# Reordering the mixer of the second block, with GpSimd multiplying its own convolution taps

## The reference

```python
h = rms_norm(x, mix_norm[l]);  u = h @ w_in[l]          # 1024 -> 2304
u_conv, u_pool = u[..., :512], u[..., 512:768]
q, k, v = jnp.split(u[..., 768:], 3, axis=-1)           # 512 each
a, gate = split(u_conv);  z = a * sigmoid(gate)          # 256 channels
z = depthwise_conv(z, w_dw, width=31) + b_dw
y_conv = silu(layer_norm(z, ln_g, ln_b))
y_pool = multiscale_pool(u_pool, pool_w[l], pool_scale[l])   # a 256x256 matrix and a 64x64 one per group
q = rms_norm(q per head of 64); k = rms_norm(k per head of 64)
p = softmax(q k^T - slope * dist)                        # 4 heads x 2 maps of 256 x 256
o = (p[:, 0] - lam * p[:, 1]) @ v
y = concat([y_conv, y_pool, rms_norm(o) * (1 - lambda_init)]) @ w_out[l]
x = x + y
```

## Time and profile before

| | |
|---|---|
| median of 3 runs | 2148.89 us (2148.51 to 2149.14) |
| the profiled execution, its own time | 2149.96 us |
| its span, first to last instruction | 2148.1 us |
| TensorE busy | 98% of the span, mean granted clock 0.992 |
| VectorE, ScalarE, GpSimd busy | 58%, 51%, 5% |
| first `mixer2` stage in the profile | 1349.8 to 1463.9 us |
| second `mixer2` stage | 1838.0 to 1952.2 us |

### The profile page before, as it was taken

One profiled execution on the slowest core, in us unless ns is written; L12 is line 12 of the kernel. 1 busy time (PEld: TensorE's weight loads), 2 busy tenths in 40 slices (PEclk: granted clock), 3 DMA queues, 4 the chain that ended last, 5 costly groups with the idle time before them and its releaser, 6 DMA issues.

```text
span 2148.1 us, 24565 instructions
## 1 busy us (share of the span) xinstructions
PE 2097.4 (98%) x9840; PEld 1730.9 (81%) x9840; DVE 1253.8 (58%) x1609; ACT 1091.8 (51%) x1554; POOL 112.6 (5%) x128
## 2 busy tenths in 40 slices
PE   7999999999999999999999999979999999979998
PEld 6888788888888887888888888868888888868886
DVE  5555666555655556665556555676555555675554
ACT  5444564544554455554446444675444444665443
POOL 1000100000000000000000000140000000140000
PEclk9999999999999999999999999989999999989999
DMA  6554635555555554455556555525554655515553
GB/s 230 194 185 162 207 125 200 177 187 185 187 191 177 194 168 147 157 181 187 186 190 224 188 193 185 171 69 175 187 190 163 224 182 185 181 65 174 179 184 120
DMA packets 104545, 379.04 MB, mean 176 GB/s; under 512 B 11745, under 2 KB 11905, under 8 KB 104176
## 3 DMA queue, kind: packets, MB, share of 16 engines
q1 hardware_dynamic: 101808, 368.23, 51.6%
q0 software_dynamic: 2080, 8.21, 1.1%
q10 hardware_dynamic: 544, 1.05, 0.2%
HBM read 374.82 MB, written 2.62 MB: 176 GB/s over the span
## 4 chain that ended last, share of the span: by engine, by line
PE 86%; issue 9%; DVE 3%; ACT 2%; DMA 0%; POOL 0%; DVEq 0%; POOLq 0%; ACTq 0%
PE pb L333 26%; PE pb L335 26%; PE pb L334 25%; DVE scr L1297 2%; PE pb L389 2%; PE pb L352 1%; PE pb L375 1%; PE pb L427 1%; PE pb L373 1%; PE pb L374 1%; DVE wlo L1287 1%; ACT scr L1142 1%; PE pb L526 0%; ACT whi L866 0%; PE pb L500 0%
## 5 line engine op out<-in xcount | busy, mean ns | idle before, releaser
L1287 DVE TENSOR_TENSOR wlo<-raw,whi 128x1024 fp32r<-128x1024 f32 (+1 forms) x704 | 839.4, 1219 | 316.3 <-ACT whi L866 312.3
L866 ACT ACTIVATE whi<-raw 128x1024 fp32r<-128x1024 f32 (+1 forms) x704 | 716.3, 1050 | 212.3 <-PE pb L335 202.9
L333 PE MATMUL pb<-whi,XTh 128*128 128x512 f32 (+2 forms) x1904 | 751.3, 395 | 4.4 <-DVE wlo L1287 4.4
L335 PE MATMUL pb<-whi,XTl 128*128 128x512 f32 (+2 forms) x1904 | 737.6, 387 | 0.0
L334 PE MATMUL pb<-wlo,XTh 128*128 128x512 f32 (+2 forms) x1904 | 736.6, 387 | 0.0
L333 PEld LDWEIGHTS pb<-whi,XTh 128*128 128x128 f32 x1904 | 359.5, 189 | 79.6 <-DVE wlo L1287 5.9
L335 PEld LDWEIGHTS pb<-whi,XTl 128*128 128x128 f32 x1904 | 359.0, 189 | 74.3
L334 PEld LDWEIGHTS pb<-wlo,XTh 128*128 128x128 f32 x1904 | 359.7, 189 | 68.2
L333 PE MATMUL pb<-whi,HTh 128*128 128x512 f32 x816 | 321.5, 394 | 8.5 <-DVE HTl L1297 8.5
L335 PE MATMUL pb<-whi,HTl 128*128 128x512 f32 x816 | 319.2, 391 | 0.0
L334 PE MATMUL pb<-wlo,HTh 128*128 128x512 f32 x816 | 319.0, 391 | 0.0
(11 more groups left out here) (209 smaller groups left out, 1117.7 us busy)
## 6 DMA issues: line engine op xcount, KB each, us to landing
raw<-in_W SPq DMA_DIRECT2D x696, 512.0 KB, 4.2
raw<-in_W SPq DMA_DIRECT2D x8, 264.0 KB, 2.7
scratch<-scr POOLq DMA_DIRECT2D x1, 1536.0 KB, 6.4
scr<-in_bc POOLq DMA_DIRECT2D x2, 640.0 KB, 5.4
X<-in_x ACTq DMA_DIRECT2D x2, 512.0 KB, 9.1
scr<-scratch POOLq DMA_DIRECT2D x1, 1024.0 KB, 7.0
scr<-in_slope POOLq DMA_DIRECT2D x1, 1024.0 KB, 9.3
scr<-in_Pg POOLq DMA_DIRECT2D x1, 1024.0 KB, 12.5
```

Of the source, the lines that this page charges most:

```text
L333: pe.matmul(o, ah, bh, start=begin and i == 0, stop=False)
L335: ins = pe.matmul(o, al, bh, start=False, stop=end and done)
L866: return act.activation(o, i, ACT.Copy, scale=scale)
L1287: dve.tensor_tensor(wlo[u % W_SLOTS][:, 0:c], raw[u % RAW_SLOTS][:, 0:c], whi[u % W_SLOTS][:, 0:c].bitcast(F32), ALU.subtract).then_inc(*u ...
```

## The change

The groups of units are now conv, q, k, pool, v, the side batches stand elsewhere, and w_out's rows are taken in the order pool, conv, attention. The taps run from k = 6 to k = 18: VectorE two or three at each step, ScalarE three at each of the steps 6 to 10 (taps 0 to 14). Taps 15 to 30 of half 1 are multiplied and added by GpSimd alone. The root of q stands on GpSimd's queue between tap 5 and tap 6, that of k between tap 14 and tap 15. The normalisation of the convolution moves from ScalarE to VectorE (`bn_stats`, `bn_aggr`, and one instruction for subtract and multiply). The core of the diff:

```diff
-OUT2 = [2, 3, 4, 5, 6, 7, 0, 1]
+OUT2 = [2, 3, 0, 1, 4, 5, 6, 7]
+ACT_TAPS = [0, 3, 6, 9, 12, 15, 15, 15, 15, 15, 15, 15, 15, 31]
+DVE_TAPS = [0, 3, 6, 8, 11, 13, 16, 18, 21, 23, 25, 27, 29, 31]
+POOL_TAPS = range(15, 31)
+POOL_AT = (6, 15)
...
 # tensor, side(k)
+                    if k == 6:
+                        turn_pair(z, ("z", i, 1), "z", 4, ("zp", i))
+                    if k == 11:
+                        turn_head(q2, "q", 0, 5)
+                        turn_head(q2, "q", 1, 6)
                     if k == 15:
+                        turn_head(k2, "k", 0, 7)
+                        turn_head(k2, "k", 1, 4)
+                        pooled(0, 5)
+                        logits(0, 0, (6, 2))
+                        logits(0, 2, (3, 7))
+                        pooled(2, 4)
+                    if k == 16:
+                        pool_groups(4)
+                        logits(1, 0, (5, 6))
                     if k == 17:
+                        turn_pair(y[:, :, 256:512], ("pool_y", i), "pool", 7, ("pool_l", i, 1))
+                        logits(1, 2, (4, 3))
                     if k == 18:
+                        turn_maps(0, 0, 5)
+                        turn_maps(0, 2, 6)
                     if k == 19:
+                        values(0, 7)
                         turn_conv(4)
                     if k == 20:
+                        turn_maps(1, 0, 5)
+                        turn_maps(1, 2, 6)
+                        turn_pair(z, ("zn", i, 1), "zn", 4, ("conv_a", i, "yc", 1))
+                        values(1, 5)
+                    if k == 21:
+                        turn_y(0, 6)
                     if k == 22:
+                        turn_y(1, 7)
+                groups = [("z", 512, 2, 4), ("qn", 512, 2, 4), ("kn", 512, 2, 4), ("up", 256, 4, 2), ("v", 512, 2, 4)]
...
 # scalar, after step(u0 + k)
+                    if 6 <= k <= 18:
+                        tap_run(ACT_TAPS[k - 6], ACT_TAPS[k - 5])
+                    if k == 7:
+                        squares(7, 2, "q_sq2")
+                    if k == 11:
+                        turned("q", qT2, gq, 0, 5)
+                        turned("q", qT2, gq, 1, 6)
+                        squares(11, 0, "k_sq2")
+                    if k == 15:
+                        turned("k", kT2, gk, 0, 7)
+                        turned("k", kT2, gk, 1, 4)
+                        pooled(0, 5)
+                        pooled(2, 4)
                         exps(0, (0, 4, 1, 5))
...
 # vector, after step(u0 + k)
+                    if 6 <= k <= 18:
+                        tap_run(DVE_TAPS[k - 6], DVE_TAPS[k - 5])
+                    if k == 8:
+                        head_mean("q")
+                    if k == 10:
+                        head_out("q", q2, 2)
+                    if k == 12:
+                        head_mean("k")
+                    if k == 14:
+                        head_out("k", k2, 0)
+                    if k == 15:
+                        maps(0, 0, (6, 2))
+                        maps(0, 2, (3, 7))
                         maps_max(0)
+                    if k == 16:
+                        maps(1, 0, (5, 6))
+                    if k == 17:
+                        # HTl of the pool's chunks
+                        maps(1, 2, (4, 3))
                         maps_max(1)
                         maps_weights(0)
                         difference(0, 0)
                         difference(0, 2)
+                    if k == 18:
                         maps_weights(1)
                         difference(1, 0)
                         difference(1, 2)
...
 # gpsimd
+                    if j in POOL_TAPS:
+                        w.wait_ge(*at("zp", i))
+                        done = one("tap_m", i, j)
+                        pool.tensor_scalar(taps[:, j % 4, :], zp[:, 1, j:j + S], cw[:, 31 + j:32 + j], None,
+                                           ALU.mult).then_inc(*done)
+                    else:
+                        w.wait_ge(*at("tap_a", i, j))
...
-                for name in ("q", "k"):
+                at_ = 1
+                for name, to in zip(("q", "k"), POOL_AT):
+                    add_taps(i, at_, to)
+                    at_ = to
                     root(col(i, "v_" + name, 16), col(i, "r_" + name, 16), 16, (name + "2_v", i, "v"), name + "2_r", i)
-                add_taps(i, 1, 25)
+                add_taps(i, at_, 31)
+                root(col(i, "v_conv", 2), col(i, "r_conv", 2), 2, ("conv_v", i, "v"), "conv_r", i)
```

More of the change, by code:

```diff
@@ L123 @@
     tensor_reduce = tensor_tensor_reduce = tensor_tensor_scan = reciprocal = memset = dma_start = op
-    wait_ge = then_inc = op
+    bn_stats = bn_aggr = wait_ge = then_inc = op
 class Once:
@@ L820, in side @@
-                    if k == 22:
[L821 to L830, removed]
+                        turn_maps(1, 0, 5)
@@ new lines, in side @@
+                        turn_maps(1, 2, 6)
[3 more added lines that the diff above has]
+                        turn_y(0, 6)
+                    if k == 22:
+                        turn_y(1, 7)
+                groups = [("z", 512, 2, 4), ("qn", 512, 2, 4), ("kn", 512, 2, 4), ("up", 256, 4, 2), ("v", 512, 2, 4)]
+                k = 0
+                for number, (emptied, ncols, per, count) in enumerate(groups):
+                    b0 = 2 * (number % 2)
+                    for j in range(count):
+                        side(k)
+                        unit(u0 + k, [(t, b0 + t, 0, ncols) for t in range(2)], XTh, XTl,
+                             [(per * j + c, c * ncols) for c in range(per)], x_ready(n), j == 0, j == count - 1)
+                        k += 1
@@ L1170, in mixer2 @@
                     if k == 3:
[L1171 to L1178, removed]
                         w.wait_ge(*at("r", n))
                         for t in range(2):
-                            w.wait_ge(*ended(u0 + 11, t))
+                            w.wait_ge(*ended(u0 + 3, t))
@@ L1193, in mixer2 @@
+                    if k == 13:
+                        for t in range(2):
+                            w.wait_ge(*ended(u0 + 13, t))
+                            scaled(up2[:, t, :], pb[2 + t][:, 0:256], n, t).then_inc(*up("up", i, t))
+                    if k == 15:
[3 more added lines that the diff above has]
+                        pooled(2, 4)
                         exps(0, (0, 4, 1, 5))
-                        tap_run(3, 5)
+                    if k == 16:
+                        w.wait_ge(*at("pool_p", i, "y"))
+                        copy(y[:, :, 256:512], pb[4][:, :].rearrange("p (t n) -> p t n", t=2)).then_inc(
+                            *up("pool_y", i))
@@ L1207, in mixer2 @@
-                    if k == 17:
-                        turned_maps(0, 0, 7)
-                        tap_run(15, 17)
+                    if k == 17:
+                        w.wait_ge(*at("pair", i, "pool"))
+                        for c in range(2):
+                            copy(HTh[:, 2 + c, :], pb[7][:, c * S:(c + 1) * S], (gp0, gp1)[c]).then_inc(
+                                *up("pool_h", i, c))
+                        exps(1, (0, 4))
                         for t in range(2):
@@ L1220, in mixer2 @@
[L1220 to L1235, removed]
-                    if k == 19:
[L1237 to L1240, removed]
-                                           accum_out=mu[:, t:t + 1]).then_inc(*up("conv_a", i, "mu", t))
@@ L1773, in mixer2 @@
+                    if k == 17:
+                        w.wait_ge(*at("pool_h", i, 1))
+                        for c in range(2):
+                            axpy(HTl[:, 2 + c, :], pb[7][:, c * S:(c + 1) * S], (gp0, gp1)[c],
+                                 HTh[:, 2 + c, :].bitcast(F32), ALU.mult, ALU.subtract).then_inc(*up("pool_l", i, c))
+                        maps(1, 2, (4, 3))
                         maps_max(1)
-                        tap_run(7, 11)
-                    if k == 16:
@@ L2084, in layout @@
         conv, pool, q, k, v = np.split(a["w_in_2"][i], [512, 768, 1280, 1792], axis=1)
+        group(conv, 2)
         group(q, 2)
         group(k, 2)
-        group(conv, 2)
+        group(pool, 4)
         group(v, 2)
-        group(pool, 4)
         group(a["w_out_2"][i].reshape(KD, P, D)[OUT2].reshape(D, D), 1)
```

167 lines of the change are left out of this document (49 added, 118 removed).

## The result

The changed kernel takes 2161.88 us in the median of four executions (2160.11 to 2164.4) against 2148.74 us for the kernel before: a ratio of 1.0062, 95% interval 1.0044 to 1.0079. It is slower by 13 us, 0.6%. The prediction was 2157.5 us, range 2141 to 2166. The profiled execution took 2161.95 us, its span 2160.1 us: 12.0 longer than the span before.

What follows compares the result with a forecast made beforehand. TensorE bounds the kernel. Per stage, stalls 23.0, half clock 3.1 and bare work 92.3 give 118.4 us against 114.1, +8.6 for two: 2157.5 us from 2148.9, range 2141 to 2166.

Steps and rivals of the forecast that it cites:

- The wait at q: New TensorE stall of 8.8 us before the q transposes at side(11), ended by VectorE's head_out of q.
- the ring: Tap slots: ScalarE's tap 10 needs tap 6's slot, which GpSimd frees only behind q's root; ScalarE stands from 27.4 until 33.2.
- rival 1: Tap slots do not hold q back: stall of 2.6 us at side(11), 2141.7 us in all, faster; chance 0.19.
- The chain of k: TensorE stalls 4.8 us before unit 14, because the v group reuses the banks of k.
- Side(18): TensorE waits for VectorE's map differences: stall of 4.2 us, and 1.0 more for pair (0, 2).
- zn and unit 20: Stage's late part: 2.4 us of stall until zn is ready, then 0.8 after silu, copy and low part.
- The half clock: TensorE work at about half clock after the stalls at q (1.7 us) and unit 14 (1.4): 3.1 a stage.
- Bare work: TensorE's own work in a stage, without stalls and half clock: 92.3 us.
- GpSimd's multiplications: 16 taps at 0.87 us each, 1.74 with the add, hidden before turn_conv with 3.9 us to spare.
- Rival 3: GpSimd becomes the bound: at 1.6 us a multiplication turn_conv waits, 5 us more a stage, 2168 us; chance 0.09.
- rival 4: VectorE's taps wait for whole GpSimd instructions: 1.33 us a tap, 2.8 more a stage, 2163 us; chance 0.06.
- Rival 2: Clock holds at unit 14 and VectorE is 2 us earlier at side(18): 2150 us, within 0.2%; chance 0.17.

Runs made afterwards that it cites:

- Experiment 1: Changed kernel with only the root of q moved on GpSimd's queue, from behind tap 5 to behind tap 9: 2154.41 us, ratio 1.0021.
- experiment 8: Changed kernel with root of q behind tap 9, separate banks for pool and v, and VectorE's head_mean and head_out before each step's taps: 2142.02 us, 0.9966.
- experiment 4: Changed kernel with VectorE's weights and map differences of row half 0 put at the start of step 17, before the taps: 2165.45 us, 1.0072.
- experiments 9 and 10: 9, on top of experiment 8: VectorE's taps and ScalarE's splits earlier, 2145.92 us; 10, on top of 9: seven GpSimd multiplications back on ScalarE, 2144.46 us.
- experiment 2: Changed kernel with idle TensorE products, 34 before the q transposes and 18 before unit 14: 2156.8 us, ratio 1.003.
- experiment 5: Changed kernel with ScalarE multiplying all taps of half 1 again and GpSimd only adding: 2162.16 us, ratio 1.0058.
- Experiment 6: Kernel before, in its own order, with GpSimd multiplying taps 15 to 30 itself: 2167.44 us, ratio 1.0078.

## Why the prediction was right, and what it mis-sized

- **The wait at q: right, the ring's share of it too large.** 8.8 us predicted, 8.63 measured in both stages; restart 40.1 us after the stage's start predicted, 40.1 measured (1390.46 by a start of 1350.35). Experiment 1 shows that the ring makes 4.1 of it, and rival 1 (the ring doesn't hold q back) is out. Even so, rival 1's stall of 2.6 us was never reached: with ring and taps out of the way (experiment 8) 3.6 us stay. By the prediction's own numbers the ring was worth 8.8 - 2.6 = 6.2 us; it measured 4.1.
- **The chain of k: right.** 4.8 predicted, 5.07 measured.
- **Side(18): the place right, the size not.** 4.2 + 1.0 predicted, 3.02 + 0.77 measured. The trace shows the predicted chain: ScalarE copies the pooled half at 1418.44, loads its table, does four exponentials and only then splits unit 19; VectorE stands 4.34 us for that split (1423.40) and then works without a break up to the differences. Which link sets the length is shown only in part: experiment 4 moved the stall by one change of VectorE's order and did not remove it, and in experiments 9 and 10 it stayed without VectorE's late taps and with fewer GpSimd instructions. ScalarE's late start fits all three; no run shortened it alone.
- **zn and unit 20: a third too large.** 2.4 + 0.8 predicted; 0.30 + 1.76 and 1.27 + 0.83 measured, 2.1 in both stages. In the first the transposes of zn did not wait at all: the 0.30 stands before `values`. `bn_stats` took 0.77 for two, 0.38 each, where the row of a map gave 0.35.
- **The half clock: the term that was mis-sized most.** In "half clock 1.7 + 1.4 = 3.1" the stall at side(18) was given none. The trace has three falls a stage: worth about 1.8, 2.2 and 3.0 us in the first (behind side(18) unit 18 takes 5.2 us in place of 2.7), and 1.4, 1.9 and 1.5 in the second. The two that were counted came near their size, as experiment 2 shows too; the third adds 2.3 a stage in the mean. The prediction gives no reason for leaving it out; what it says of the clock is inferred from one stall, "it fell at about 4.8 us of idling", and beside that a stall of 4.2 looks safe. (The 0.55 of that row puts the fall at 4.6 us.) In the windows above it fell 2.0 us into the q stall, 2.6 into the k stall, and 0.5 us behind the 3.02 at side(18). In the second stage it fell 4.5 us into the same 8.63 us stall at q (the row of 1877.70). So one stall's figure could not serve as a limit.
- **Bare work: 2 us a stage too small.** 92.3 in the sum, 94.3 to 94.9 in the four stages of the table. The residual transposes in the stage's tail are missing from it, 0.79 (1469.80 to 1470.59), and the first product behind each side batch costs 0.31 to 0.34 to the next and not 0.23 (1418.33 to 1418.67 to 1418.90), some ten times, about 1 us. This error is worth 4.2 us over both stages and has its opposite in the stalls, 2.7 a stage too large. The second stage of before was taken as long as the first, but is 1.5 us longer, which flattered the change by that much.
- **GpSimd's multiplications: right.** 0.92 against an estimated 0.87 each, 1.83 for multiplication and add against 1.74; the last add ends at 1437.04 and `turn_conv` comes at 1443.82. Rival 3 is out, and experiment 5 shows that the cover holds. Experiment 6 shows what it costs without cover.
- **Taps beside GpSimd: right.** 1.81 us for two at 1387.27, near the 0.87 that the sum took and not the 1.33 of rival 4. The rule behind it (the Trainium skill, SBUF — State Buffer, Who interferes with whom) is seen better from GpSimd's side: the multiplication of 1424.07 took 1.78 us in place of 0.92 while VectorE's split of two SBUF inputs ran.
- **Rival 2, a milder clock and milder later stalls:** the stall at side(18) was indeed 1.4 and 1.7 us shorter, but the clock went the other way.

The sum, by these terms: the gaps came to 5.4 us less than predicted over the two stages, the half clock to 5.6 more, the bare work to 4.2 more, rounding aside: 241.1 us of stages against 236.8. That the total came out near is in part luck. With the stalls at their measured size and the other two terms as predicted it would have been 231.4, only 3.2 us above the 228.2 that the prediction took for before, which is no change by its own measure of 4.3. The direction rests on the stalls at q and k, and these came in the predicted place and near the predicted size.

## What to carry to other kernels

When an in-order engine (here GpSimd) gets a long instruction ahead of the consumer of a small ring, look past its own finish: the engine that fills the ring stops, and what is queued behind the fill, here a weight split and then a finished head, is late. Reordering whole groups moves such waits rather than removing them, so search for the one instruction whose place holds the ring (experiment 1: one number, 9 of the 13 us lost) before judging the order. And sum a stage as gaps, half clock and bare work, and check that the three give the stage of the kernel before; here that check would have shown the bare work 2 us short and the second stage longer.

## What the runs showed of the hardware that was not expected

- The granted clock fell from 1.00 to 0.5 at very different points of stalls: 2.0 and 2.6 us into those at q and k in the changed kernel's first stage, 4.5 us into the one at q in its second, 4.6 us into the long one of before, and 0.5 us after the end of a 4.5 us stall in experiment 1. In experiment 8 a stall of 3.6 us at q was followed by a fall in the second stage and by none in the first, where the fall came 1.2 us behind the later stall of 1.77 us. Behind each of these falls 2.7 to 4.4 us of work ran at half clock.
- Idle products are a usable cover: 12 us of them in each stage, placed inside the stalls, made the changed kernel 7 us faster.
- A GpSimd multiplication by a per-partition scalar (128x256) took 0.92 us where its two-input add of the same size took 0.73: one input less wasn't cheaper. The Trainium skill (GPSIMD Engine Reference, Engine selection) calls one-input work roughly line-rate and two-input work about two times slower than VectorE's; these two rows show no such order.
